# Attention on TensorE: units taken in mirrored pairs, and a compressed branch padded to the tiles of the value products

## The reference

```python
s_c = einsum(q, kc) - slope * d_c;   o_c = einsum(masked_softmax(s_c), vc)   # compressed keys, one per 16 positions, 31 of them
s_s = einsum(q, k_sel) - slope * d_s; o_s = einsum(masked_softmax(s_s), v_sel)  # selected blocks
s_w = einsum(q, k_win) - slope * d_w; o_w = einsum(masked_softmax(s_w), v_win)  # window
o = g[0] * o_c + g[1] * o_s + g[2] * o_w
```

## Time and profile before

| | us |
|---|---|
| median of 3 runs | 1969.65 |
| lowest and highest | 1965.89, 1969.80 |
| profiled execution | 1977.36 |
| its span, first to last instruction | 1974.8 |
| TensorE busy in the span | 1823.2 (92%) |
| VectorE busy | 683.8 (35%) |
| ScalarE busy | 513.5 (26%) |

### The profile page before, as it was taken

One profiled execution on the slowest core, in us unless ns is written; L12 is line 12 of the kernel. 1 busy time (PEld: TensorE's weight loads), 2 busy tenths in 40 slices (PEclk: granted clock), 3 DMA queues, 4 the chain that ended last, 5 costly groups with the idle time before them and its releaser, 6 DMA issues.

```text
span 1974.8 us, 52583 instructions
## 1 busy us (share of the span) xinstructions
PE 1823.2 (92%) x23219; PEld 1451.0 (73%) x23219; DVE 683.8 (35%) x1812; ACT 513.5 (26%) x1199; POOL 100.7 (5%) x155
## 2 busy tenths in 40 slices
PE   5999999999988898999998899999999989999993
PEld 3776777777776577899987754686666778999982
DVE  5241135666664333111113500406777231111105
ACT  2112223333331112111111200315777231111103
POOL 2111000000000002000001000000000001000002
PEclk9999999999998998999999999898999998999996
DMA  8665744433333487999979991633000286999944
GB/s 297 189 221 195 255 147 124 132 105 110 101 112 114 127 250 296 356 414 416 416 307 235 229 184 72 197 85 87 2 1 2 56 351 242 383 412 417 416 167 155
DMA packets 195381, 413.47 MB, mean 209 GB/s; under 512 B 53686, under 2 KB 135314, under 8 KB 186674
## 3 DMA queue, kind: packets, MB, share of 16 engines
q1 hardware_dynamic: 176386, 357.95, 52.7%
q0 software_dynamic: 11040, 39.85, 5.7%
q10 hardware_dynamic: 7760, 12.79, 1.8%
HBM read 356.84 MB, written 57.91 MB: 210 GB/s over the span
## 4 chain that ended last, share of the span: by engine, by line
PE 48%; issue 7%; DVE 3%; ACT 2%; DMA 2%; DVEq 1%; POOL 0%; ACTq 0%; SPq 0%
PE bank L1985 11%; PE bank L1980 6%; PE bank L1998 5%; PE bank L2004 4%; PE bank L1707 3%; PE bank L2852 3%; PE bank L2960 2%; PE bank L2908 2%; PE bank L2997 2%; PE bank L1962 1%; PE bank L1973 1%; DMA rows<-y_slots,pos 1%; PE bank L2784 1%; PE bank L2929 1%; PE bank L2085 1%
## 5 line engine op out<-in xcount | busy, mean ns | idle before, releaser
L1980 PE MATMUL bank<-wg,slot_x 128*32 128x384 f32 x1056 | 123.0, 504 | 4.1 <-ACT slot_x L2172 2.7
L1985 PE MATMUL bank<-wg,slot_x 128*32 128x128 f32 x1056 | 124.4, 280 | 0.0
L1980 PE MATMUL bank<-wu,slot_x 128*32 128x384 f32 x1056 | 119.0, 486 | 3.9 <-issue 3.9
L1985 PE MATMUL bank<-wu,slot_x 128*32 128x128 f32 x1056 | 119.3, 273 | 0.0
L1998 PE MATMUL bank<-wd,actT 128*32 128x384 f32 x1056 | 117.5, 486 | 1.4 <-ACT actT L2195 1.4
L2004 PE MATMUL bank<-wd,actT 128*32 128x256 f32 (+1 forms) x704 | 118.1, 326 | 0.0
L1985 PEld LDWEIGHTS bank<-wg,slot_x 128*32 128x32 f32 x1056 | 116.7, 113 | 1.2
L1985 PEld LDWEIGHTS bank<-wu,slot_x 128*32 128x32 f32 x1056 | 115.2, 110 | 2.3
L640 PE MATMUL bank<-xm,wp 128*128 128x272 f32 x480 | 113.3, 395 | 0.0
L640 PEld LDWEIGHTS bank<-xm,wp 128*128 128x128 f32 x480 | 90.2, 190 | 20.6 <-issue 2.7
L2400 DVE TENSOR_TENSOR act<-bank,act 128x384 f32<-128x384 f32 x32 | 17.9, 558 | 249.2 <-PE bank L1985 249.2
(11 more groups left out here) (632 smaller groups left out, 4038.5 us busy)
## 6 DMA issues: line engine op xcount, KB each, us to landing
wg<-in_moe_w_gate_dram SPq DMA_DIRECT2D x22, 2048.0 KB, 11.5
wu<-in_moe_w_up_dram SPq DMA_DIRECT2D x22, 2048.0 KB, 16.3
wd<-in_moe_w_down_dram SPq DMA_DIRECT2D x22, 2048.0 KB, 11.5
xT<-in_ada_w_dram SPq DMA_DIRECT2D x40, 1024.0 KB, 5.6
w<-in_moe_w_gate_dram SPq DMA_DIRECT2D x10, 2048.0 KB, 11.6
fT<-in_moe_w_up_dram SPq DMA_DIRECT2D x10, 2048.0 KB, 16.1
gall<-in_moe_w_down_dram SPq DMA_DIRECT2D x10, 2048.0 KB, 11.2
wp<-in_rwkv_w_rkv_dram SPq DMA_DIRECT2D x24, 512.0 KB, 4.6
```

The costliest lines, as they stand in the source:

```text
L1980: mm = pe.matmul(ps[32 * j:32 * j + 32, 0:GW], x[:, k, 32 * j:32 * j + 32], w[:, k, 0:GW], start=k == 0, stop=k == KT - 1)
L1985: mm = pe.matmul(ps[96:128, q * 128:(q + 1) * 128], x[:, kk, 32 * q:32 * q + 32], w[:, kk, GW:FF], start=kk == 0, stop=kk == KT - 1)
```

## The change

The diff does five things.

1. PE's loop takes two units in an iteration, in mirrored order: scores(s), turn(s-4), values(s-6), values(s-5), turn(s-3), scores(s+1). The next iteration begins with scores(s+2).
2. The compressed branch is padded. `B.vcp` has its own 64 columns for each h and zeros in all other rows, so its value product takes all 128 rows. The compressed turn loads 64 columns, from `B.scc_flat`, of which 33 are those of the next block. ACT copies bank 6 in one instruction.
3. `NSC` goes from 5 to 4, and there are three `B.PT` (`NPT = 3`); the third lies where the fifth `B.sc` was.
4. ACT takes the copies of unit s-4 in its step s, and stores a head's output one step later.
5. DVE clears `B.vcp` once ahead of the compression and `B.scc_flat` once ahead of attention.

```diff
@@ allocate_nsa
-    B.vcp = sb(kv, "vcp", [128, 2, HD])
+    B.vcp = sb(kv, "vcp", [128, 2, 2, HD])
-    B.PT = [view(A, at + i * 1024, 2, 512) for i in range(2)]
+    B.PT = [view(A, at + i * 1024, 2, 4, 128) for i in range(2)] + [B.kvtok[:, 0:2, 0:512].rearrange("p h (k t) -> p h k t", t=128)]
+    B.scc_flat = view(A, at + 872, 2 * 248 + 64 - NCP)
-    B.sc = [view(A, i * 1024, 2, 512) for i in range(3)] + [B.kvtok[:, 2 * i:2 * i + 2, 0:512] for i in range(2)]
+    B.sc = [view(A, i * 1024, 2, 512) for i in range(3)] + [B.kvtok[:, 2:4, 0:512]]
-NSC = 5
+NSC = 4
+NPT = 3
@@ pe_attend, cmp_turn and values
-                mm = pe.matmul(bank[6][64 * h:64 * h + NCP, i * 128:(i + 1) * 128], B.scc[j % 2][:, h, i, :], ident[:], start=True, stop=True)
+                c = (8 * (j % 2) + 4 * h + i) * NCP
+                mm = pe.matmul(bank[6][hs(h), i * 128:(i + 1) * 128], B.scc_flat[:, c:c + 64], ident[:], start=True, stop=True)
-                rows = slice(64 * h, 64 * h + NCP)
-                pe.matmul(o[h], B.vcp[rows, j // HG, :], B.PTc[j % 2][rows, i * 128:(i + 1) * 128], start=True, stop=False)
+                pe.matmul(o[h], B.vcp[:, j // HG, h, :], B.PTc[j % 2][:, i * 128:(i + 1) * 128], start=True, stop=False)
@@ pe_attend, the loop
-    for s in range(NA + 4):
-        if s < NA:
-            ...
-            scores(s)
-        if 3 <= s and s - 3 < NA:
-            turn(s - 3)
-            ...
-        if s >= 4:
-            values(s - 4)
+    for s in range(0, NA + 6, 2):
+        step_scores(s)
+        step_turn(s - 4)
+        step_values(s - 6)
+        step_values(s - 5)
+        step_turn(s - 3)
+        step_scores(s + 1)
@@ act_kv
-    for s in range(NA + 3):
-        if s % 8 == 4 and s > 8:
+    for s in range(NA + 4):
+        if s % 8 == 5 and s > 8:
             act_store_heads(act, B, s // 8 - 1)
-        if s >= 3:
-            u = s - 3
-            if u >= 2:
-                act.wait_ge(S("pv_mm"), u - 1)
+        if s >= 4:
+            u = s - 4
+            if u >= NPT:
+                act.wait_ge(S("pv_mm"), u - NPT + 1)
-                for h in range(2):
-                    rows = slice(64 * h, 64 * h + NCP)
-                    ins = act.activation(B.PTc[j % 2][rows], bank[6][rows, :], ACT.Copy)
-                ins.then_inc(S("ptc_ev"), 1)
+                act.activation(B.PTc[j % 2], bank[6], ACT.Copy).then_inc(S("ptc_ev"), 1)
@@ dve_kv and dve_attend
+    dve.memset(B.vcp[:], 0.0)
-        ins = dve.tensor_copy(B.vcp[rows].rearrange("p g d -> p (g d)"), bank[6][rows, 256:256 + 2 * HD])
+        ins = dve.tensor_copy(B.vcp[rows, :, h, :], bank[6][rows, 256:256 + 2 * HD].rearrange("p (g d) -> p g d", g=2))
+    dve.memset(B.scc_flat, 0.0)
+    dve.drain()
```

More of the change, by code:

```diff
@@ L2567, in allocate_nsa @@
     B.pair = sb(kv, "pair", [128, 64])
-    sb(kv, "spare", [128, 232])
+    sb(kv, "spare", [128, 104])
     b_ = sb(kv, "region_b", [128, 16 * 512])
@@ L2964, in sample_values @@
         bq, gp = SUNITS[u - NU]
-        PT = B.PT[u % 2]
+        PT = B.PT[u % NPT]
         o = bank[6 + gp][:, bq * 128:(bq + 1) * 128]
@@ L2968, in sample_values @@
             pe.wait_ge(S("o_ev"), KT)
-        pe.matmul(o, PT[0:NCK, 0, 384:512], B.vcs[:, 2 * gp:2 * gp + 2, :].rearrange("p g d -> p (g d)"), start=True, stop=False)
+        pe.matmul(o, PT[0:NCK, 0, 3], B.vcs[:, 2 * gp:2 * gp + 2, :].rearrange("p g d -> p (g d)"), start=True, stop=False)
         for br in range(2):
@@ L2972, in sample_values @@
                 for b in range(4):
-                    at = kt * 128 + 32 * b
-                    pe.matmul(o[32 * b:32 * b + 32], PT[:, br, at:at + 32], B.vp[br][:, 2 * (4 * bq + b) + kt, gp * 128:(gp + 1) * 128],
+                    pe.matmul(o[32 * b:32 * b + 32], PT[:, br, kt, 32 * b:32 * b + 32], B.vp[br][:, 2 * (4 * bq + b) + kt, gp * 128:(gp + 1) * 128],
                               start=False, stop=False)
             v = (3 + 2 * br) * 256 + gp * 128
-            mm = pe.matmul(o, PT[0:NS, br, 256:384], B.kvtok[0:NS, 4, v:v + 128], start=False, stop=br == 1)
+            mm = pe.matmul(o, PT[0:NS, br, 2], B.kvtok[0:NS, 4, v:v + 128], start=False, stop=br == 1)
         mm.then_inc(S("pv_mm"), 1)
@@ L2996, in values, with step_scores, step_turn, step_values @@
                 v = (3 + 2 * br) * 256 + (2 * (j // HG) + h) * HD
-                mm = pe.matmul(o[h], B.kvtok[:, kt, v:v + HD], B.PT[u % 2][:, h, kt * 128:(kt + 1) * 128], start=False, stop=br == 1 and kt == i)
+                mm = pe.matmul(o[h], B.kvtok[:, kt, v:v + HD], B.PT[u % NPT][:, h, kt], start=False, stop=br == 1 and kt == i)
         mm.then_inc(S("pv_mm"), 1)
-    for s in range(NA + 4):
-        if s < NA:
-            first = s < NU and UNITS[s][1:] == (0, 0)
-            if first:
-                cmp_scores(UNITS[s][0], 0)
-            scores(s)
-            if first:
-                cmp_scores(UNITS[s][0], 1)
-        if 3 <= s and s - 3 < NA:
-            turn(s - 3)
-            if s - 3 < NU and UNITS[s - 3][1:] == (0, 0):
-                cmp_turn(UNITS[s - 3][0])
-        if s == NU + 4:
+    def step_scores(u):
+        if u >= NA:
+            return
+        first = u < NU and UNITS[u][1:] == (0, 0)
+        if first:
+            cmp_scores(UNITS[u][0], 0)
+        scores(u)
+        if first:
+            cmp_scores(UNITS[u][0], 1)
+    def step_turn(u):
+        if not 0 <= u < NA:
+            return
+        turn(u)
+        if u < NU and UNITS[u][1:] == (0, 0):
+            cmp_turn(UNITS[u][0])
+    def step_values(u):
+        if not 0 <= u < NA:
+            return
+        if u == NU:
             pe.wait_ge(S("vp_loaded"), 272)
             pe.wait_ge(S("ptc_ev"), KT)
-        if s >= 4:
-            values(s - 4)
+        values(u)
+    for s in range(0, NA + 6, 2):
[5 more added lines that the diff above has]
+        step_scores(s + 1)
     for gp in range(2):
@@ L3073, in act_kv @@
                    bank[0][:, 0:256].rearrange("p (n a c) -> p a n c", n=2, a=2)[:, :, :, 0:48], ACT.Copy).then_inc(S("q_ev"), 1)
-    for s in range(NA + 3):
-        if s % 8 == 4 and s > 8:
+    for s in range(NA + 4):
+        if s % 8 == 5 and s > 8:
             act_store_heads(act, B, s // 8 - 1)
-        if s >= 3:
-            u = s - 3
+        if s >= 4:
+            u = s - 4
             j, i, br = UNITS[u] if u < NU else (None, None, None)
-            if u >= 2:
-                act.wait_ge(S("pv_mm"), u - 1)
+            if u >= NPT:
+                act.wait_ge(S("pv_mm"), u - NPT + 1)
             for h in range(2):
-                w = 128 * (i + 1) if u < NU else (512, 384)[h]
+                n = i + 1 if u < NU else 4 - h
                 act.wait_ge(S("pt_tr"), 2 * u + h + 1)
-                act.activation(B.PT[u % 2][:, h, 0:w], bank[4 + h][:, 0:w], ACT.Copy).then_inc(S("pt_ev"), 1)
+                act.activation(B.PT[u % NPT][:, h, 0:n], bank[4 + h][:, 0:128 * n].rearrange("p (k t) -> p k t", t=128), ACT.Copy)\
+                   .then_inc(S("pt_ev"), 1)
             if (i, br) == (0, 0):
                 act.wait_ge(S("ptc_tr"), j + 1)
-                for h in range(2):
-                    rows = slice(64 * h, 64 * h + NCP)
-                    ins = act.activation(B.PTc[j % 2][rows], bank[6][rows, :], ACT.Copy)
-                ins.then_inc(S("ptc_ev"), 1)
+                act.activation(B.PTc[j % 2], bank[6], ACT.Copy).then_inc(S("ptc_ev"), 1)
         if s < NU:
```

## The result

| | before | after |
|---|---|---|
| median of 14 runs each | 1970.0 us | 1961.12 us |
| profiled execution: span | 1974.8 us | 1962.5 us |
| a head, start to start (heads 3 to 5) | 22.18 us | 20.70 us |
| attention stage, first compressed score to first output projection | 203.8 us | 195.6 us |

What follows compares the result with a forecast made beforehand. TensorE bounds the attention stage, and afterwards the loop through TensorE, VectorE and ScalarE. Heads -10.7, first head +0.9 and tail +0.75 sum to -9.0 us, 1960.7 us; own range 1956 to 1965, overall range 1949 to 1970.

Steps and rivals of the forecast that it cites:

- The fixed price belongs to the tile shape: TensorE, attention stage: changing the array's tiles costs 0.155 us, 0.21 behind scores, whatever the semaphore waits; 4.9 us per head.
- remainder: Time on TensorE beyond streaming at a change of shape: 0.155 us behind turns and value products, 0.21 behind scores.
- TensorE alone would need 19.2 us: A head on TensorE's own work after saving 2.95 us by order, padding and the wait for bank 7.
- Half comes back as two waits, in these places, with these causes: Per head, TensorE waits for ScalarE's copies, 0.66 us at the turn of unit 3, 0.9 at unit 0's; period 20.65.
- the chain: One head's instructions followed in order through TensorE, VectorE and ScalarE: period 20.65 us, 1.53 below 22.18.
- The wait for bank 7, 0.88, goes by the new order: Before a head's first values: ScalarE's store now comes between the last value pair and the next head's first, saving 0.88 us.
- First head, 0.9 lost: First head: scores of unit 4 wait ahead of the turns, so unit 5's come later, 0.9 us lost (bounds 0 and 2).
- Tail, 0.75 lost: Last four units (samples): turn of unit 66 waits about 0.9 us, shape changes return 0.15; 0.75 lost (bounds 0 and 2).
- TensorE alone: Rival, attention stage: VectorE and ScalarE keep up, so TensorE alone decides; 1950 us, range 1947 to 1955, chance 0.18.
- Slower by the clock: Rival: new waits inside a head drop TensorE to 1.2 GHz; one 3 us stretch per head gives some 1976 us; chance 0.09.
- No change: Rival: remainder no matter of tiles, or loop through VectorE and ScalarE 1.5 us longer; 1966 to 1973 us, chance 0.15.

Runs made afterwards that it cites:

- the last kernel: Changed kernel with ScalarE's copies of odd units, unit 2 and the first sample unit one step earlier, last store moved: 19.15 us a head, 0.9858 of the kernel before.
- order-only kernel: Changed kernel with the compressed branch taken back to unpadded, with two copies and no memsets: 20.98 us a head, 0.9966 of the kernel before.
- the one with more work on VectorE: Changed kernel with one more 64-column copy and drain on VectorE in each prompt unit: 21.62 us a head, 0.9984 of the kernel before.
- the one with unit 2's copy: Changed kernel with ScalarE's copy of a head's unit 2 ahead of the exponential of unit 5: 20.27 us a head, 0.9911 of the kernel before.
- padding-only kernel: Kernel before with only the compressed branch padded, one copy of bank 6 and the memsets, old order: 20.75 us a head, ratio 0.9940.
- one-copy kernel: Kernel before with ScalarE copying bank 6 in one instruction instead of two: 21.31 us a head, ratio 0.9982.

## Why the prediction was right

*The fixed price belongs to the tile shape.* Shown. C, V, V have one remainder in place of three, with the same waits on semaphores between them; the kernel with the padding alone lost them in the old order. The Trainium skill's rule that a change of tiling mode drains TensorE ("TensorEngine Tiling (Array Packing)", Key Properties) agrees, and has its number here: 0.155 us, 0.21 behind the scores. V to T measured 0.17 and T to S 0.16, where 0.18 and 0.17 were taken. Padding took away 0.71 us a head, where 0.77 was taken: between C and V up to 0.06 are left (0.27 us for records that stream in 0.21), and 0.07 behind CT. Not each change of the tiles that the profile names has the price: in the sample units of the kernel before, transposes at 128*32 and 128*120 follow full ones at 0.11 us a record and nothing more (1535.18 to 1535.83). What sets them apart from CT was not tested.

*TensorE alone would need 19.2 us.* Shown by the kernel with both copies moved, 19.15.

*Half comes back as two waits, in these places, with these causes.* Shown: 0.65 before T3 (0.97 from 1396.61 to 1397.58, against 0.32 in the last kernel), forecast 0.66; 0.81 before and in T0 (1.81 - 1.28, and 0.28), forecast 0.9; both released by ScalarE's copies. The period was 20.70, forecast 20.65. VectorE's idle before the scores of unit 5 was 1.72, forecast some 2. A third wait of 0.18 before T6 I had at zero. The order-only kernel (20.98), the one with more work on VectorE (21.62) and the one with unit 2's copy (20.27) come out near what the chain gives when it is worked out anew, and away from the sum of work.

*The wait for bank 7, 0.88, goes by the new order.* It went, but this step credited the order with what the padding's single copy does as well. It goes in either way: by the order (no such wait in the order-only kernel, with its two copies) or by the single copy (21.31 in the kernel before). The parts do not add: padding alone 1.43 of a head, order alone 1.20, together 1.48. In time the padding, which I had at 0.77, is worth the whole change in a head, and its stage is even 2.5 us shorter than the changed kernel's, 2.3 of them in the tail (35.25 us from the end of the last S5, against 37.55). The mirrored order pays only once ScalarE's copies are moved: then 1.6 us a head beyond the padding.

*First head, 0.9 lost.* None was: the end of S5 came 12.80 us after the first compressed score before and 12.79 after. What was forecast did happen. S4 stands ahead of the turns and waits for VectorE, and the compressed turn ran at the lower level, 1.2 GHz (16 records in 1.98 us; PEclk is 0.50 in 1345 to 1350):

```profile
1347.93 1.65 PE L2910 MATMUL bank<-kT,region_a 64*128 64x384 f32 x4 [1.90 <-DVE region_a L3263]
...
1350.13 1.98 PE L2940 MATMUL bank<-ident,region_a 128*64 128x128 f32 x16
```

But the head began with fast records where that of before began with slow ones (the clock had fallen 1.1 us later), and VectorE was 0.8 us ahead when it took the scores of unit 2. So the comparison with the kernel before is luck in part. The padding-only kernel, in the old order and with the clock falling as late as in the changed one, has the end of S5 at 12.63 us: against that one 0.16 is lost, and not 0.9. What the draw of the clock is worth is more than the whole term: in the one-copy kernel, with 17 us at 0.50, the end of S5 came after 14.8 us.

*Tail, 0.75 lost.* The end of S5 of the last head to the output projection took 35.7 us before and 37.55 after: 1.87 lost. The mechanism was right and the size short by one wait: T65 waits as well, 0.96, for the copy of unit 64, which ScalarE has behind the exponential of unit 67, and T66 then 0.51, where 0.9 was taken:

```profile
1521.69 0.41 PE L2948 MATMUL bank<-ident,region_a 128*128 128x128 f32 x2 [0.96 <-ACT region_a L3101]
...
1523.16 0.41 PE L2948 MATMUL bank<-ident,region_a 128*128 128x128 f32 x2 [0.51 <-ACT kvtok L3101]
```

Together: seven heads of 1.48 and one 0.34 longer, 10.0 (forecast 10.7), no loss ahead (0.9), 1.87 behind (0.75): 8.2 against 9.0. The errors of the two ends nearly cancel, so part of the closeness of the total is luck; the heads, 10.0 against 10.7, are not.

*The rivals.* TensorE alone: fell, 20.70 and not 19.2 a head, though the busy shares of three quarters spoke for it. Slower by the clock: fell, the granted clock is 1.00 in each stretch from 1355 us to the end of the stage, with idle of 0.46 and 0.59 in each head. No change: fell.

## What to carry to other kernels

Where three engines hand a unit round, add up each engine's work, and then follow one round of instructions in their order: the sum gave 19.2 us and missed half of the answer, the chain gave 20.65 and measured 20.70. An engine that idles a tenth of its time can still set the pace, if an instruction that waits for a late engine stands ahead of one that is ready; reordering that queue was worth as much again (1.55 us a head) as the change itself (1.48).
Array shapes have a price at each change, so a small product that streams no longer when padded is best given the shape of its neighbours, even with most rows zero. And judge an edit's parts alone as well: here two of them removed the same wait.

## What was not expected of the hardware

A copy of bank 6 over 128 rows takes ScalarE 0.60 us (1391.61 in the changed kernel), as long as one over 31 rows (0.59, half of the 1.19 above): two copies of parts cost twice the copy of the whole. And the value product streams as fast with 128 rows as with 31 (4 records are busy 0.44 and 0.43 us), as the prediction had taken from V's rows, so zeros cost nothing there.

One of the steady heads of most mirrored kernels is longer, 21.04 instead of 20.70 in the changed kernel (1440.51 to 1461.55), with 0.78 of idle before T0 instead of 0.46. VectorE's rows show where it comes from:

```profile
1392.45 0.62 DVE L3290 TENSOR_SCALAR kvtok<-kvtok,region_a 128x256 f32<-128x256 f32 x2 [0.42 <-issue]
```

```profile
1446.09 0.88 DVE L3290 TENSOR_SCALAR kvtok<-kvtok,region_a 128x512 f32<-128x512 f32 x2 [0.42 <-issue]
```

VectorE stands still for 0.42 us twice in the steady part, with nothing in the profile that it waits for. The first time is just ahead of its long idle before the scores of unit 5, and the head keeps its length. The second time is in the chain that leads to T0: each of VectorE's instructions up to there comes 0.33 us late, and so does T0. The other kernels have the same pauses of 0.38 to 0.43 us, and their longer heads are those in which one falls into that chain; in the three kernels of the old order no head shows one. That is the loop once more, tried by a delay that no edit put there. What makes VectorE pause stays open.
